# Five probability tiles turned through DRAM instead of two, and half of the weight loads issued by ScalarE, in a two-layer hybrid attention trunk

## The reference

```python
h = rms_norm(x, pre_w)
proj = h @ w_in                       # 1024 x 4680
dq, dk, dv, dg, sq, sk, sv, sg, iq, ik, iw = split(proj)
# group A, differential attention, per head two 64-wide maps c = 0, 1
p = softmax(where(causal, dq_c @ dk_c.T * 64 ** -0.5, -inf))
oa = rms_norm((p[0] - lam * p[1]) @ dv, subln_w) * (1 - lambda_init) * silu(dg)
# group B, sparse attention, keys chosen by an indexer (64 of the causal ones per query)
score = sum_h relu(iq_h @ ik.T) * iw_h
p = softmax(where(chosen by top_k(score), sq @ sk.T * 128 ** -0.5, -inf))
ob = (p @ sv) * silu(sg)
x = x + rms_norm(concat(oa, ob) @ w_out, post_w)
```

## Time and profile before

| | |
|---|---|
| three runs | 302.51, 303.12, 303.51 us, median 303.12 |
| the profiled execution | 302.85 us, its span 301.1 us |
| granted TensorE clock, mean | 0.996 of full speed |
| busy, us | PE 292.4, PEld 246.4, DVE 234.9, ACT 163.9, POOL 67.6 |
| DMA | 60.01 MB, 62229 packets, 34560 of them under 512 B |

### The profile page before, as it was taken

One profiled execution on the slowest core, in us unless ns is written; L12 is line 12 of the kernel. 1 busy time (PEld: TensorE's weight loads), 2 busy tenths in 40 slices (PEclk: granted clock), 3 DMA queues, 4 the chain that ended last, 5 costly groups with the idle time before them and its releaser, 6 DMA issues.

```text
span 301.1 us, 4401 instructions
## 1 busy us (share of the span) xinstructions
PE 292.4 (97%) x1568; PEld 246.4 (82%) x1568; DVE 234.9 (78%) x474; ACT 163.9 (54%) x284; POOL 67.6 (22%) x116
## 2 busy tenths in 40 slices
PE   8999999999999999999999999999999999999992
PEld 7799777788787888788888988778878788887892
DVE  4752989899999997955984786878999999787343
ACT  5986963736577473603665855473737747390101
POOL 6558210303030220101060740012303030210101
PEclk9999999999999999999999999999999999999998
DMA  7999959457518569860059799937653675742011
GB/s 242 370 371 386 371 214 354 135 143 227 195 69 210 209 211 303 191 201 23 0 158 369 242 350 250 325 108 204 209 150 131 146 272 152 202 70 72 0 70 70
DMA packets 62229, 60.01 MB, mean 199 GB/s; under 512 B 34560, under 2 KB 39424, under 8 KB 62208
## 3 DMA queue, kind: packets, MB, share of 16 engines
q1 hardware_dynamic: 61920, 59.47, 62.8%
q10 hardware_dynamic: 288, 0.26, 0.3%
HBM read 54.48 MB, written 5.24 MB: 198 GB/s over the span
## 4 chain that ended last, share of the span: by engine, by line
PE 40%; DVE 37%; ACT 8%; DMA 6%; POOL 4%; issue 3%; SPq 1%; POOLq 0%; DVEq 0%; ACTq 0%
DVE w_lo L987 14%; PE bank_a L470 8%; PE bank_a L461 7%; PE bank_a L466 7%; PE bank_s L618 6%; DMA w_raw<-in_w_in 6%; PE bank_a L618 5%; ACT xt_pbuf L831 4%; DVE work L1107 4%; DVE xt_pbuf L1124 3%; DVE top L1106 3%; DVE xt_pbuf L1140 3%; DVE mixn L1150 2%; DVE mixn L1036 2%; PE bank_s L559 1%
## 5 line engine op out<-in xcount | busy, mean ns | idle before, releaser
L987 DVE TENSOR_TENSOR w_lo<-w_raw,w_hi 128x2048 fp32r<-128x2048 f32 (+1 forms) x46 | 98.8, 2154 | 18.5 <-ACT w_hi L763 18.3
L763 ACT ACTIVATE w_hi<-w_raw 128x2048 fp32r<-128x2048 f32 (+1 forms) x46 | 81.9, 1784 | 31.9 <-PE bank_a L470 23.4
L461 PE MATMUL bank_a<-w_hi,h_hi 128*128 128x512 f32 (+1 forms) x272 | 72.5, 388 | 0.0
L470 PE MATMUL bank_a<-w_lo,h_hi 128*128 128x512 f32 (+1 forms) x272 | 70.0, 379 | 0.5 <-DVE w_lo L987 0.5
L466 PE MATMUL bank_a<-w_hi,h_lo 128*128 128x512 f32 (+1 forms) x272 | 69.9, 379 | 0.0
L470 PEld LDWEIGHTS bank_a<-w_lo,h_hi 128*128 128x128 f32 x272 | 49.7, 188 | 10.5 <-DVE w_lo L987 1.0
L466 PEld LDWEIGHTS bank_a<-w_hi,h_lo 128*128 128x128 f32 x272 | 49.8, 188 | 9.8
L461 PEld LDWEIGHTS bank_a<-w_hi,h_hi 128*128 128x128 f32 x272 | 47.9, 188 | 10.4 <-issue 2.7
L831 ACT ACTIVATE xt_pbuf<-xt_pbuf,st 128x128 f32<-128x128 f32 (+1 forms) x48 | 21.3, 444 | 25.1 <-DVE st L1124 25.1
L1417 POOL TENSOR_TENSOR rt<-nat,tab 128x256 f32<-128x256 f32 x10 | 7.4, 741 | 112.5 <-ACT nat L815 112.5
L815 ACT ACTIVATE nat<-bank_a,st 128x512 f32<-128x512 f32 x20 | 13.5, 681 | 19.6 <-PE bank_a L470 19.6
(11 more groups left out here) (196 smaller groups left out, 431.1 us busy)
## 6 DMA issues: line engine op xcount, KB each, us to landing
w_raw<-in_w_in SPq DMA_DIRECT2D x30, 1024.0 KB, 6.0
w_raw<-in_w_out SPq DMA_DIRECT2D x8, 1024.0 KB, 6.1
w_raw<-in_w_in SPq DMA_DIRECT2D x8, 584.0 KB, 7.3
turned<-mixn SPq DMA_DIRECT2D x20, 128.0 KB, 2.7
prm<-in_rows SPq DMA_DIRECT2D x2, 705.0 KB, 7.0
w_raw<-in_w_in SPq DMA_DIRECT2D x2, 512.0 KB, 6.3
xres<-in_x SPq DMA_DIRECT2D x2, 512.0 KB, 9.5
dqT<-turned SPq DMA_DIRECT2D x2, 512.0 KB, 5.9
```

The source lines that it names most:

```text
L461: pe.matmul(bank, h_hi[:, HALF * half + kk, tok], whi[:, kk, :], start=half == 0 and kk == 0, stop=False)
L470: mm = pe.matmul(bank, h_hi[:, HALF * half + kk, tok], wlo[:, kk, :], start=False, stop=half == 1 and kk == HALF - 1)
L763: act.activation(unit(w_hi, u), unit(raw, u), ACT.Copy).then_inc(hi_done.sem, 1)
L987: dve.tensor_tensor(unit(w_lo, u), unit(raw, u), unit(w_hi, u).bitcast(F32), ALU.subtract).then_inc(lo_done.sem, 1)
```

## The change

1. TensorE's 12 transposes per layer of PD0, PD1A and PD1B go away, with their three drains. VectorE turns these tiles in 32 x 32 squares (`turn_probs(PD0, 6)` and so on), into parts of `mixn` and `nat` that are free; SyncE writes them to DRAM in four pieces each and reads them back into `pT`. The squares of SQ go to `iqT` instead of `mixn`.
2. SyncE's queue issues the weight loads of units up to 15 only (`SP_UNITS = 12`). From then on the queue holds the puts and gets of DQ, SQ, PD0, PD1A, PD1B, PS0, PS1, one after another. The loads of units 16 to 23, and units 0 to 3 of the next layer, are issued by ScalarE (`fetch(u)`: wait for `split_lo(u)`, issue unit u + 4), between its own instructions.
3. The order is changed. TensorE: `values(0)` two half groups later, `values(1)` after `second(18)`, `values(2)` after the first `out_part`, the turns MS0 and MD1 together after the second, then `values(3)`, then the parts of half 1. VectorE: `split_lo(20)` to `(22)` come later, `gate_dsa(0)` before `split_lo(22)`, MS0 is drained before MD1. ScalarE: `move(15)` before `exps(10)` and `exps(11)`.
4. Buffers of the turned tiles are declared flat; the tiles' places in them are the same.

```diff
@@ -54,6 +54,7 @@
 UNITS = IN_UNITS + 4
 GROUPS = BLOCKS * CHUNKS
 RING = 4
+SP_UNITS = 12
...
-T_IK, T_DK, T_PD0, T_PD1A, T_SK, T_PD1B = 4, 5, 7, 8, 9, 11
-T_MD0, T_MD1, T_MS0, T_MS1 = 12, 13, 14, 15
-T_USES = 16
-PS0, PS1 = range(3, 5)
+T_IK, T_DK, T_SK = 4, 5, 7
+T_MD0, T_MS0, T_MD1, T_MS1 = 9, 10, 11, 12
+T_USES = 13
+IQS, DQS, SQS, PD0, PD1A, PD1B, PS0, PS1 = range(8)
+SLOT = {PD0: 0, PD1A: 1, PD1B: 2, PS0: 0}
...
@@ -173,7 +175,7 @@
         subln = st[:, 152:153]
         rd, rs = st[:, 154:156], st[:, 156:158]
         squares = mixn[:, :, :].rearrange("p b n -> p (b n)")
-        prob_buf = {PS0: dkT[:, 0:2, :].rearrange("p f t -> p (f t)"), PS1: dqT[:, :, :, :].rearrange("p b f t -> p (b f t)")}
+        prob_buf = {PD0: mixn[:, 0, :], PD1A: nat[:, 1, 0, :], PD1B: nat[:, 1, 1, :], PS0: dkT[:, 0:2, :].rearrange("p f t -> p (f t)"), PS1: dqT[:, :]}
...
                 first(14)
                 second(14)
                 first(15)
-
-                pe.wait_ge(combined.sem, combined.at(layer, 1))
-                turn_probs(T_PD0, 6, 0, HEADS)
                 diff_scores(10, 1, (2, 3))
                 second(15)
-
-                pe.wait_ge(combined.sem, combined.at(layer, 2))
-                turn_probs(T_PD1A, 8, 1, 2)
                 first(16)
                 second(16)
                 turn_nat(T_SK, 0, 5)
                 first(17)
 
-                pe.wait_ge(combined.sem, combined.at(layer, 3))
-                turn_probs(T_PD1B, 10, 1, 2)
-
                 pe.wait_ge(t_drained.sem, t_drained.at(layer, T_SK + 2))
                 pe.wait_ge(sq_landed.sem, sq_landed.at(layer, sq_landed.per_layer))
                 dsa_scores(12, 0, range(HEADS))
-                pe.wait_ge(t_drained.sem, t_drained.at(layer, T_PD0 + 1))
-                values(0, 0, v_diff, [[slot(0, h)] for h in range(HEADS)], place(layer, DV, 0) + 1)
                 second(17)
                 first(18)
+
+                pe.wait_ge(prob_landed[PD0].sem, prob_landed[PD0].at(layer, 16))
+                values(0, 0, v_diff, [[gathered(pT[:, 0, :], h, slots=HEADS)] for h in range(HEADS)], place(layer, DV, 0) + 1)
                 dsa_scores(13, 1, (0, 1))
                 dsa_scores(14, 1, (2, 3))
-                pe.wait_ge(t_drained.sem, t_drained.at(layer, T_PD1B + 1))
-                values(1, 1, v_diff, [[slot(1 + h // 2, 2 * (h % 2) + t) for t in range(2)] for h in range(HEADS)],
+                second(18)
+
+                pe.wait_ge(prob_landed[PD1A].sem, prob_landed[PD1A].at(layer, 16))
+                pe.wait_ge(prob_landed[PD1B].sem, prob_landed[PD1B].at(layer, 16))
+                values(1, 1, v_diff, [[gathered(pT[:, 1 + h // 2, :], 2 * (h % 2) + t, slots=HEADS) for t in range(2)] for h in range(HEADS)],
                        place(layer, DV, 1) + 1)
-                second(18)
+                first(19)
                 turn_mix(T_MD0, 0, 0)
-                first(19)
                 second(19)
-                turn_mix(T_MD1, 1, 1)
-
-                pe.wait_ge(prob_landed[PS0].sem, prob_landed[PS0].at(layer, 16))
-                values(2, 0, v_dsa, [[slot(0, h)] for h in range(HEADS)], place(layer, SV, 0) + 1)
-
+
+                pe.wait_ge(proj_moved.sem, proj_moved.at(layer, place(layer, SV, 0) + 1))
                 pe.wait_ge(t_drained.sem, t_drained.at(layer, T_MD0 + 1))
                 out_part(0, 0, 0)
-                turn_mix(T_MS0, 0, 2)
+
+                pe.wait_ge(prob_landed[PS0].sem, prob_landed[PS0].at(layer, 16))
+                values(2, 0, v_dsa, [[gathered(pT[:, 0, :], h, slots=HEADS)] for h in range(HEADS)], place(layer, SV, 0) + 1)
 
                 pe.wait_ge(proj_moved.sem, proj_moved.at(layer, GROUPS))
                 out_part(0, 0, 1)
+                turn_mix(T_MS0, 0, 2)
+                turn_mix(T_MD1, 1, 1)
+
+                pe.wait_ge(prob_landed[PS1].sem, prob_landed[PS1].at(layer, 16))
+                values(3, 1, v_dsa, [[gathered(pT[:, 1:3, :].rearrange("p s n -> p (s n)"), 2 * h + t) for t in range(2)] for h in range(HEADS)],
+                       place(layer, SV, 1) + 1)
 
                 pe.wait_ge(t_drained.sem, t_drained.at(layer, T_MS0 + 1))
                 out_part(1, 0, 0)
-
-                pe.wait_ge(prob_landed[PS1].sem, prob_landed[PS1].at(layer, 16))
-                values(3, 1, v_dsa, [[slot(1 + h // 2, 2 * (h % 2) + t) for t in range(2)] for h in range(HEADS)],
-                       place(layer, SV, 1) + 1)
                 out_part(1, 0, 1).then_inc(y_done.sem, 1)
...
+            def fetch(layer, u):
+
+                act.wait_ge(lo_done.sem, lo_done.at(layer, u + 1))
+                to = (layer, u + RING) if u + RING < UNITS else (layer + 1, u + RING - UNITS)
+                if to[0] < DEPTH:
+                    act.dma_start(unit(raw, to[1]), weights(*to)).then_inc(raw_landed[u % RING].sem, 16)
...
@@ -896,14 +889,18 @@
                 relu(5)
                 move(9)
                 split_hi(layer, 13)
+                fetch(layer, 12)
                 move(10)
                 split_hi(layer, 14)
+                fetch(layer, 13)
                 move(11)
                 act.wait_ge(lam_summed.sem, lam_summed.at(layer, 1))
                 act.activation(lam_e, lam_s, ACT.Exp).then_inc(lam_exped.sem, 1)
                 split_hi(layer, 15)
                 move(12)
+                fetch(layer, 14)
                 split_hi(layer, 16)
+                fetch(layer, 15)
                 exps(6, 0, 4)
                 exps(7, 0, 4)
                 move(13)
@@ -912,25 +909,33 @@
                 exps(9, 1, 2)
                 move(14)
                 split_hi(layer, 18)
+                fetch(layer, 16)
+                move(15)
                 exps(10, 1, 2)
                 exps(11, 1, 2)
-                move(15)
                 split_hi(layer, 19)
+                fetch(layer, 17)
                 move(16)
                 split_hi(layer, 20)
                 exps(12, 0, 4)
+                fetch(layer, 18)
                 move(17)
                 square_o(0)
                 split_hi(layer, 21)
+                fetch(layer, 19)
                 exps(13, 1, 2)
                 exps(14, 1, 2)
                 square_o(1)
+                fetch(layer, 20)
                 move(18)
                 split_hi(layer, 22)
                 move(19)
                 split_hi(layer, 23)
+                fetch(layer, 21)
                 square_y(0, 0)
                 square_y(0, 1)
+                fetch(layer, 22)
+                fetch(layer, 23)
...
                 def turn_probs(n, use):
-                    dve.wait_ge(exps_done.sem, exps_done.at(layer, use + 1 - S_DIFF0))
-                    probs = pbuf[:, 0, :] if n == PS0 else pbuf[:, 1:3, :].rearrange("p s n -> p (s n)")
+                    if n >= PS0:
+                        dve.wait_ge(exps_done.sem, exps_done.at(layer, use + 1 - S_DIFF0))
+                    else:
+                        dve.wait_ge(combined.sem, combined.at(layer, n - PD0 + 1))
+                    probs = pbuf[:, 1:3, :].rearrange("p s n -> p (s n)") if n == PS1 else pbuf[:, use % 4, :]
                     dve.transpose(prob_buf[n], probs).then_inc(prob_squares.sem, 1)
...
@@ -1248,43 +1256,42 @@
 
                 mask_scores(8, 1, 2, causal[:, :])
                 mask_scores(9, 1, 2, causal[:, :])
+                turn_squares(1, 4, sq_squares.sem)
                 dve.wait_ge(dq_put.sem, dq_put.at(layer, 16 * SQUARES))
-                turn_squares(1, 4, sq_squares.sem)
+                turn_probs(PD0, 6)
                 split_lo(layer, 16)
                 combine(8, 1, 2, 0)
-
-                drain(T_PD0, pT[:, 0, :])
+                dve.wait_ge(sq_squares.sem, sq_squares.at(layer, 1))
+                turn_probs(PD1A, 8)
+
                 mask_scores(10, 1, 2, causal[:, :])
                 mask_scores(11, 1, 2, causal[:, :])
                 split_lo(layer, 17)
+                combine(10, 1, 2, 2)
+                turn_probs(PD1B, 10)
+
+                dve.wait_ge(sq_put.sem, sq_put.at(layer, 16 * SQUARES))
+                drain_pair(T_SK, skT)
                 choose(1, 2)
-                drain(T_PD1A, pT[:, 1, :])
-                combine(10, 1, 2, 2)
+                mask_scores(12, 0, 4, work[0][:, :])
+                split_lo(layer, 18)
                 choose(1, 1)
                 mask_unchosen(1)
-                drain_pair(T_SK, skT)
-                split_lo(layer, 18)
-
-                drain(T_PD1B, pT[:, 2, :])
-                mask_scores(12, 0, 4, work[0][:, :])
+                turn_probs(PS0, 12)
                 split_lo(layer, 19)
-                turn_probs(PS0, 12)
-                split_lo(layer, 20)
-
-                gate_diff(0)
-                split_lo(layer, 21)
                 mask_scores(13, 1, 2, work[1][:, :])
                 mask_scores(14, 1, 2, work[1][:, :])
-
+                gate_diff(0)
+                split_lo(layer, 20)
```

(6 more changed lines are left out.)

108 lines of the change are left out of this document (50 added, 58 removed).

## The result

| | before | changed |
|---|---|---|
| median (lowest to highest), us | 302.98 (302.51 to 303.51) | 317.14 (315.37 to 318.61) |
| runs | 4 | 4 |
| ratio to before (95% interval) | 1 | 1.0465 (1.0441 to 1.0489) |
| profiled execution: time, span | 302.85, 301.1 | 316.57, 314.8 |
| mean granted TensorE clock | 0.996 | 0.979 |

The change makes the kernel slower by 4.65%. The forecast was 299.5.

What follows compares the result with a forecast made beforehand. TensorE, busy 97% of the span, was taken as the bound, so fewer instructions shorten it. Per layer 1.42 + 0.69 - 0.3 = 1.8, twice 3.6, off 302.85 gives 299.25; plus 0.27 for the median, 299.5 us; range 298.4 to 302.3.

Steps and rivals of the forecast that it cites:

- Transposes of TensorE: TensorE: three groups of transposes fewer (PD0, PD1A, PD1B), saving 1.42 us per layer, all on the path.
- The stall at MS0: TensorE's turn MS0 no longer waits for VectorE's gate, saving 0.69 us per layer.
- VectorE's splits: VectorE: `split_lo(17)` ends at 98.1, wanted by TensorE at 98.15; cost between nothing and 0.1, taken as nothing.
- The new stall of 0.3 at `split_lo(23)`: VectorE late in the layer: `split_lo(23)` ends at 134.3, 0.3 us after TensorE's out_part wants it, per layer.
- ScalarE's fetches: Weight-load issues on ScalarE, 0.45 each, covered by its idle time; taken as nothing, 2 us without that cover.
- SyncE's chain: SyncE's queue: puts of 5.1 each, PD1B's get lands at 112.8, `values(1)` wants it at 114.6: slack 1.8.
- my bound above, 6.8: SyncE's queue: with 6.8 for both PD1A's and PD1B's puts, the get lands at 116.2, late by 1.6.
- SQ's get "still at 94.8": SyncE's queue: SQ's get is issued at 94.8, as before the change.
- The slow rival: Small pieces run one after another; PD1B's get lands at 119.5, 4.9 late; 309.3 in full; chance 0.13.
- PS1: SyncE's queue: PS1's get lands at 128.2 or 130.3, wanted at 129.5; slack 1.3 taken, not late by 0.8.

Runs made afterwards that it cites:

- the fastest kernel: Changed kernel, but ScalarE issues only the loads of units 20 to 23, after PD1B's put; next layer's four on SyncE's queue behind PS1's get: 300.98 us, ratio 0.9944.

## Why the prediction was wrong

- **Transposes of TensorE**: right. L440 on xt_pbuf is gone, and in the fastest kernel the gain of a layer comes to 2.04 by starts, with the next term in it (forecast 1.42 + 0.69).
- **The stall at MS0**: right, no turn waits for the gate in the changed kernel; it is part of the same 2.04.
- **VectorE's splits**: right that it just holds, but it cost 0.2 in each layer, over the bound of 0.1 and taken as nothing. `split_lo(17)` was to end at 98.1, with TensorE's four matmuls wanting it at 98.15. VectorE's timeline of the changed kernel has it at 95.70 for 2.29, and the matmuls start at 98.04, but take 1.14 to the next start instead of 0.91:

```profile
95.70 2.29 DVE L992 TENSOR_TENSOR w_lo<-w_raw,w_hi 128x2048 fp32r<-128x2048 f32 x1
```

- **The new stall of 0.3 at `split_lo(23)`**: right in place and size where `values(3)` does not wait: in layer 1 of the changed kernel, and in both layers of the one with one load held (0.31, 0.32). TensorE's timeline in the former:

```profile
294.47 1.20 PE L610 MATMUL bank_a<-w_hi,h_hi 128*128 128x512 f32 x4 [0.32 <-DVE w_lo L992]
```

- **ScalarE's fetches**: an issue takes 0.37 instead of 0.45 and delays no exponential. But "on SyncE nothing queues behind a late weight any more" counted only one direction. I asked what a load does to the queue that it leaves, and not beside which puts it would then run.
- **The failed step, SyncE's chain**: "I take 5.1, because in the new program no weight load stands in this queue, as none stood ahead of SQ's put, and the pieces are half its size." PD1B's put took 8.51 and SQ's, which I had left where it was, 9.07. The pieces were indeed no trouble: PD1B's put takes 4.1 to 4.4 with no load beside it in the changed order (4.9 and 5.3 in one layer each of two kernels). The inference from rows 6 was the fault. Of the trace behind them I had read that SQ's 5.1 had no load ahead of it in its queue, and that PS0's 6.8 had loads ahead of and between its pieces. The second is wrong: none stands between the pieces (110.26 to 113.78), only one just ahead (109.64) and one behind (113.82). And there is no case at all of a load in the other queue. I took that missing case for the better of the two, and my bound above, 6.8, was the other end of what I had seen, not of what could be. Measured, it is 7.6 to 10.6 with one or two such loads issued from just ahead of the put to the end of its issue.
- **SQ's get "still at 94.8"**: it came at 98.62. A put on which the change touched nothing but the neighbours got no bound at all. Nor did its get: it took 6.1 and 6.2 to land, and with the 3.3 of the kernel without loads beside it, it would by my estimate have landed at 101.9, before TensorE was ready at 102.9. The two late starts of the scores are 4.7 of the 11.0 that the listed starts of the scores and of `values(1)` lost.
- **The slow rival** put the break at the right place (PD1B's get late at `values(1)`), through small pieces run one after another. It forecast 119.5 for the landing, close to the 120.5 that came, by luck and the wrong cause: with the same pieces and no loads beside them `values(1)` starts on time. 13% was too little for it: the price of a put beside the other queue's loads was unknown from above. Its 309.3 missed SQ's place and the clock.
- **PS1**: the forecast took a slack of 1.3 and set "late by 0.8" aside; it was late by 0.5 in layer 0 of the changed kernel and by 0.9 in the fastest.
- **The clock** was in no term. 5.0 us of the loss are matmuls at a lower granted clock behind stalls.

## What to carry to other kernels

Before moving loads to another queue, list which transfers with short runs and a reader close behind would then have a load beside them, and price them by a trace that shows that pair; a queue's order counts, not only its length. Price the get behind the put in the same way. Let bulk loads start behind the last get that somebody is waiting for, and check what the split behind the load holds up. Price a stall of TensorE with what follows it at the lower clock.

## What the runs showed of the hardware

- A half-megabyte put in runs of 128 bytes (SQ, PS1) takes 5.4 to 5.6 with no load beside it, and 5.1 (before) to 5.6 (all loads on one queue) with a load right behind it in its own queue. With a load ahead in its own queue it takes 5.7 (3.6 ahead) to 9.9, and 8.4 to 9.9 when the load is 0.5 ahead. With one or two loads of 1 MB from the other queue, issued while its pieces are issued, it takes 8.3 to 10.2; with such loads only ahead of it, 5.9 (3.3 ahead) to 8.8 (1.6 ahead); with three from 1.6 before its start on, 14.9. One such load costs SQ's put 3.4 (the kernel before with ScalarE's loads) to 3.6 (the one load held).
- Puts of half that size (PD1B, PS0) took 4.1 to 5.3 with no load beside them, 7.6 to 10.6 with one or two of the other queue's, and 8.7 and 11.9 in the fastest kernel, with three. How the packets interleave stays open.
- SQ's get of 512 KB lands 3.3 to 3.7 after its issue (once 4.3) with no load shortly ahead of it, 5.3 to 7.2 with one issued 0.6 to 2.6 ahead, in either queue.
- The granted clock stayed 1.00 behind waits of 1.81 (104.8 to 109.0 in the changed kernel) and of 2.48 (128.5 to 133.0 with PS1's put first), and was 0.62 behind 3.74, 0.57 behind 2.60, 0.67 behind 2.25 and 0.62 behind 2.00 (273.9 to 278.4, the same execution as the 2.48). So the length of the wait alone does not decide it.
- SQ's put late by 3.4 and PS1's by 3.6 cost 0.3% in the order of before. In the changed order the same lateness of SQ's put stops TensorE for 1.81 and 2.60: the order before had slack where the new one has none. The larger part of the loss, at `values(1)`, hangs on PD1B's tile, which did not go through DRAM before.
